# Second layer's modulation: products on TensorE, or a running sum over row tiles on VectorE

## The reference, cut to what matters

```python
for l in range(DEPTH):                               # DEPTH = 2, D = 1024
    mod = silu_c @ w_mod[l] + b_mod[l]               # w_mod[l]: 1024 x 6144
    mod_c = silu_cc @ w_mod[l] + b_mod[l]
    sh1, sc1, g1, sh2, sc2, g2 = jnp.split(mod[:, None, :], 6, axis=-1)
    csh1, csc1, cg1, csh2, csc2, cg2 = jnp.split(mod_c, 6, axis=-1)
    ac = modulate(rms_norm_2(hc, norm1_g[l]), csh1, csc1)
    ...
    h = h + g1 * mix
    h = h + g2 * sq_relu_mlp(modulate(rms_norm_2(h, norm2_g[l]), sh2, sc2), w_ff1[l], w_ff2[l])
    if l < DEPTH - 1:                                # the context leaves after layer 0
        hc = hc + cg1 * mix_c
        ...
```

## Time and profile before

| | us |
|---|---|
| median of 3 timed runs | 2056.79 |
| range of the runs | 2055.26 to 2058.39 |
| span of the profiled execution | 2050.1 |
| TensorE busy in the span | 1990.1 |
| VectorE busy | 1195.2 |
| ScalarE busy | 890.0 |

### The profile page before, as it was taken

One profiled execution on the slowest core, in us unless ns is written; L12 is line 12 of the kernel. 1 busy time (PEld: TensorE's weight loads), 2 busy tenths in 40 slices (PEclk: granted clock), 3 DMA queues, 4 the chain that ended last, 5 costly groups with the idle time before them and its releaser, 6 DMA issues.

```text
span 2050.1 us, 33804 instructions
## 1 busy us (share of the span) xinstructions
PE 1990.1 (97%) x13960; PEld 1728.6 (84%) x13960; DVE 1195.2 (58%) x2137; ACT 890.0 (43%) x1514; POOL 167.0 (8%) x187
## 2 busy tenths in 40 slices
PE   7899999999999999999999999999999999999998
PEld 7768999897889999787788877777778897997887
DVE  6756666776466666425434455444444635677776
ACT  5656544436464444325423333222232426455443
POOL 0220100012021100003410000000000003000000
PEclk9999999999999999899999999999999999999999
DMA  7374699856656665225433325455444421664554
GB/s 233 100 225 146 182 224 224 213 173 188 203 153 180 187 209 164 62 59 163 129 102 93 104 72 185 144 183 165 151 144 153 136 77 37 188 193 144 185 185 134
DMA packets 331751, 317.60 MB, mean 155 GB/s; under 512 B 17077, under 2 KB 315964, under 8 KB 331342
## 3 DMA queue, kind: packets, MB, share of 16 engines
q1 hardware_dynamic: 326580, 301.64, 48.3%
q0 software_dynamic: 3904, 12.03, 2.9%
q10 hardware_dynamic: 1114, 1.76, 0.3%
HBM read 306.54 MB, written 8.85 MB: 154 GB/s over the span
## 4 chain that ended last, share of the span: by engine, by line
PE 87%; DVE 6%; DMA 3%; ACT 2%; issue 1%; POOL 0%; ACTq 0%; SPq 0%; DVEq 0%; POOLq 0%
PE acc L673 20%; PE acc L674 19%; PE acc L675 19%; PE acc L723 7%; PE acc L722 4%; DVE w_low L1963 3%; PE pss L872 2%; PE acc L688 1%; PE acc L719 1%; PE acc L689 1%; PE acc L690 1%; DMA raw<-in_w_mod 1%; PE pst L884 1%; ACT w_high L1421 1%; DMA raw<-in_l_w_down 1%
## 5 line engine op out<-in xcount | busy, mean ns | idle before, releaser
L1963 DVE TENSOR_TENSOR w_low<-raw,w_high 128x1024 fp32r<-128x1024 f32 (+4 forms) x503 | 561.5, 1156 | 151.9 <-ACT w_high L1421 149.3
L1421 ACT ACTIVATE w_high<-raw 128x1024 fp32r<-128x1024 f32 (+4 forms) x503 | 471.9, 984 | 393.8 <-PE acc L675 242.7
L673 PE MATMUL acc<-normed,w_high 128*128 128x256 f32 (+1 forms) x1768 | 568.7, 322 | 0.2
L674 PE MATMUL acc<-normed,w_high 128*128 128x256 f32 (+1 forms) x1768 | 563.4, 319 | 0.0
L675 PE MATMUL acc<-normed,w_low 128*128 128x256 f32 (+1 forms) x1768 | 562.9, 318 | 0.0
L673 PEld LDWEIGHTS acc<-normed,w_high 128*128 128x128 f32 x1768 | 338.4, 191 | 28.7 <-issue 4.4
L675 PEld LDWEIGHTS acc<-normed,w_low 128*128 128x128 f32 x1768 | 338.5, 191 | 22.8
L674 PEld LDWEIGHTS acc<-normed,w_high 128*128 128x128 f32 x1768 | 338.6, 192 | 22.3
L723 PE MATMUL acc<-inner,w_high 128*128 128x512 f32 x612 | 218.1, 396 | 0.0
L673 PE MATMUL acc<-inner,w_high 128*128 128x512 f32 (+2 forms) x576 | 199.2, 346 | 2.2 <-DVE w_low L1963 2.0
L674 PE MATMUL acc<-inner,w_high 128*128 128x512 f32 (+2 forms) x576 | 196.7, 341 | 0.0
(11 more groups left out here) (278 smaller groups left out, 2783.6 us busy)
## 6 DMA issues: line engine op xcount, KB each, us to landing
raw<-in_w_ff SPq DMA_DIRECT2D x128, 512.0 KB, 4.3
raw<-in_w_mod SPq DMA_DIRECT2D x96, 512.0 KB, 4.8
raw<-in_w_in SPq DMA_DIRECT2D x84, 512.0 KB, 4.1
raw<-in_l_w_gate SPq DMA_DIRECT2D x44, 512.0 KB, 5.2
raw<-in_l_w_up SPq DMA_DIRECT2D x44, 512.0 KB, 4.4
raw<-in_l_w_down SPq DMA_DIRECT2D x32, 512.0 KB, 4.7
raw<-in_l_w_qkv SPq DMA_DIRECT2D x24, 512.0 KB, 4.4
raw<-in_l_w_out SPq DMA_DIRECT2D x16, 512.0 KB, 4.6
```

The source lines that it names most:

```text
L673: mm(dst, lh, rh, start=i == 0, stop=False)
L674: mm(dst, lh, rl, start=False, stop=False)
L1421: nc.scalar.activation(WH[:, s % NSPLIT, w0:w0 + nw], RAW[:, r:r + nw], ACT.Copy).then_inc(w_high, 1)
L1963: V.tensor_tensor(WL[:, s % NSPLIT, c], RAW[:, r:r + nw], WH[:, s % NSPLIT, c].bitcast(F32), ALU.subtract).then_inc(w_low, 1)
```

## The change

Layer 0's modulation stays as it is. Layer 1's is computed in another way, in the same stage.

- The loads: `w_mod[1]` now comes as rows. A piece is one row tile (128 rows, one per partition) by 1024 columns, which is one of the six parts `q` (shift 1, scale 1, gate 1, shift 2, scale 2, gate 2). There are 32 late units, one after every ordinary unit of the stage. The first 16 have one piece each (parts 0 and 1, eight row tiles each), the last 16 have two (parts 2 to 5). That is 48 pieces and 25 MB, as before.
- VectorE: for each piece it multiplies the row by the vector's value of that partition and adds it to a running sum in fp32 of 128 by 1024 (L2186 for row tile 0, L2189 for the others). Parts 0 and 1 have two sums, one per vector, parts 2 to 5 one. A piece is free when its last such operation is done.
- TensorE: when a part is complete, at the earliest two units later, each 128 columns of the sum are the stationary operand against one column of ones, which sums over the partitions and leaves the result as a column in `PSO` (`late_columns`, L837): 16 matmuls for parts 0 and 1, 8 for parts 2 to 5. VectorE adds the bias into `MODC` (L2202).
- Gone from the stage: the 24 units of `modulate`, the 12 `columns`, ScalarE's 12 copies and VectorE's 12 reductions with their bias additions.

```diff
+        def mod_sum(q, s):
+            return wk(D * q, D) if s else (view(ROPE, 0, (D,)) if q % 2 == 0 else wk(2 * D, D))
...
-        mod_units = [(l, c) for l in range(2) for c in range(0, 6 * D, 256)]
+        mod_units = [(0, c) for c in range(0, 6 * D, 256)]
...
+        def late_modulation():
+            q, j = (len(late_mods) // 8, len(late_mods) % 8) if len(late_mods) < 16 else \
+                (2 + (len(late_mods) - 16) // 4, 2 * ((len(late_mods) - 16) % 4))
+            n = 1 if q < 2 else 2
+            unit(part(kp(A["w_mod_2"][1])[:, j:j + n, D * q:D * q + D], 0, D), words=n * D, split=False)
+            late_mods.append((q, j, n))
+            ahead.append(len(order) - 1)
...
                     for m in range(0, D, cols):
                         unit(part(kp(A["w_ff2_2"][l])[:, tiles * c:tiles * (c + 1), m:m + cols], 0, cols))
-                        if l == 0 and m == 0:
-                            modulation(1)
-                            ahead.append(len(order) - 1)
+                        if l == 0:
+                            late_modulation()
...
+            def late_columns(steps):
+                while st["late"] < sum(end <= steps - 2 for end in mod_end):
+                    q = st["late"]
+                    if q:
+                        pe.wait_ge(mod_known, q)
+                    pe.wait_ge(mod_added, mod_ready[q])
+                    for s in range(2 if q < 2 else 1):
+                        for c in range(KD):
+                            ins = mm(PSO[:, KD * s + c:KD * s + c + 1], mod_sum(q, s)[:, P * c:P * c + P], ones[:, 0:1],
+                                     start=True, stop=True)
+                    ins.then_inc(mod_summed, 1)
+                    st["late"] += 1
...
                 def step():
                     if l == 0:
-                        modulate((PSO, PSS[0]), PSS[1])
+                        assert not order[st["unit"]][0]
+                        st["unit"] += 1
+                        st["steps"] += 1
+                        late_columns(st["steps"])
...
+            def late_modulation():                     # on VectorE, after each unit's split()
+                q, j, n = late_mods[st["late"]]
+                u = ahead[st["late"]]
+                late_known(sum(end <= st["late"] - 4 for end in mod_end))
+                st["late"] += 1
+                for i in range(len(pieces[u])):
+                    dve.wait_ge(w_full[landed[u, i][0]], landed[u, i][1])
+                    w = RAW[:, raw_at[u, i]:raw_at[u, i] + D]
+                    for s in range(2 if q < 2 else 1):
+                        acc, part = mod_sum(q, s), SILC[:, j + i, s:s + 1]
+                        if j + i == 0:
+                            ins = V.tensor_scalar(acc, w, part, None, ALU.mult)
+                        else:
+                            dve.wait_ge(mod_added, st["added"] - (q < 2))
+                            ins = V.scalar_tensor_tensor(acc, w, part, acc, ALU.mult, ALU.add)
+                        st["added"] += 1
+                        ins.then_inc(mod_added, 1)
+                    raw_free[u, i] = (mod_added, st["added"])
...
+            def late_known(upto):
+                while st["known"] < upto:
+                    q = st["known"]
+                    st["known"] += 1
+                    dve.wait_ge(mod_summed, q + 1)
+                    bm = vcol["b_mod_2"] + 48 + KD * q
+                    for s in range(2 if q < 2 else 1):
+                        ins = V.tensor_tensor(MODC[:, 48 + KD * q:48 + KD * q + KD, s], PSO[:, KD * s:KD * s + KD],
+                                              VEC[:, bm:bm + KD], ALU.add)
+                    ins.then_inc(mod_known, 1)
+                    dve.wait_ge(mod_known, q + 1)
...
                             for i in range(4):
                                 residual_half(2 * i, 48 * l + 40, 0)
                                 if i == 1:
-                                    modulation(len(mod_units) // 2 - 1)
-                            modulation(len(mod_units) // 2)
+                                    late_modulation()
+                            late_modulation()
+                            late_known(5)
                             residual_half(0, 48 * l + 40, 1)
```

More of the change, by code:

```diff
@@ L317, in build @@
         MODS = 8
+        late_mods = []
+        def late_modulation():
[5 more added lines that the diff above has]
+            ahead.append(len(order) - 1)
         FFN_CHUNKS = [(0, 8), (8, 8), (16, 6)]
@@ L389, in build @@
                         unit(part(kp(A["w_ff2_2"][l])[:, tiles * c:tiles * (c + 1), m:m + cols], 0, cols))
-                        if l == 0 and m == 0:
-                            modulation(1)
-                            ahead.append(len(order) - 1)
-        assert len(mod_used) == len(mod_units)
+                        if l == 0:
+                            late_modulation()
+        assert len(mod_used) == len(mod_units) and late_mods[-1] == (5, 6, 2)
         split_ids = [i for i, u in enumerate(order) if u[0]]
@@ L553, in build @@
         skew_w = sem("skew_w")
+        mod_added, mod_summed, mod_known = sem("mod_added"), sem("mod_summed"), sem("mod_known")
         bias_in = sem("bias_in")
@@ L566, in build @@
         raw_free = {}
+        mod_ready = [16, 32, 40, 48, 56, 64]
+        mod_end = [sum(q <= p for q, j, n in late_mods) for p in range(6)]
         pair_bank, cols_bank = {}, {}
@@ L632, in _ @@
             st = {"phase": 0, "acc": 0, "unit": 0, "split": 0, "task": 0, "sq": 0, "freed": 0, "store": 0,
-                  "pair": 0, "rope": 0, "spread": 0}
+                  "pair": 0, "rope": 0, "spread": 0, "late": 0, "steps": 0}
             mm = nc.tensor.matmul
@@ L996, in last_product @@
                 turned(wb, four, x, 4, S)
-                all_columns()
+                step()
                 turned(wa, four[0:2], far, 4, S)
@@ L1009, in last_product @@
                 split_free[a] = (acc_full, st["acc"])
-                turned(wb, four, far, 4, S)
+                turned(wb, four[0:2], far, 4, S)
+                late_columns(len(late_mods) + 2)
+                turned(wb, four[2:4], far, 4, S)
                 split_free[b] = (acc_full, st["acc"])
@@ L1308, in _ @@
                                 project(1, hidden(c, T), T, m=cols // P, kt=tiles)
-                            if m == 0:
-                                step()
+                            step()
                             if last and m:
@@ L1855, in _ @@
                 tiles = 2048 // T
-                steps = 2 * st["pair"]
                 for kind, c in ffn2_turns(T):
@@ L1859, in _ @@
                         for m in range(0, tiles, 2):
-                            if l == 0:
-                                modulation_rows((steps - 1) // 2)
-                                steps += 1
                             if l:
@@ L1935, in _ @@
             st = {"phase": 0, "chain": 0, "acc": 0, "task": 0, "rot": 0, "sig": 0, "split": 0, "store": 0, "mod": 0,
-                  "relu": 0, "turned": 0, "spread": 0}
+                  "relu": 0, "turned": 0, "spread": 0, "late": 0, "added": 0, "known": 0}
             go = lambda: fence(dve, st)
@@ L2071, in mod_gain @@
                 m = 48 * l + 24 * which + 8
-                for s in range(2):
+                for s in range(1 if l and which else 2):
                     link(V.scalar_tensor_tensor(MGAIN[:, which, :, s], MODC[:, m:m + 8, s], 1.0,
@@ L2591, in _ @@
                 tiles = 2048 // T
-                steps = 2 * st["mod"]
                 for kind, c in ffn2_turns(T):
-                    if l == 0 and kind == "out":
-                        modulation((steps - 2) // 2)
-                        steps += 1
                     if kind == "in":
                         for m in range(0, tiles, 2):
-                            if l == 0:
-                                modulation((steps - 2) // 2)
-                                steps += 1
                             if l:
@@ L2650, in _ @@
                             residual_half(4, 48 * l + 40, 1)
+                            late_known(6)
                             residual_half(6, 48 * l + 40, 1)
```

8 lines of the change are left out of this document (removed).

## The result

The changed kernel takes 2070.45 us (2068.98 to 2073.46, 4 runs) against 2057.59 before (2055.26 to 2058.5, 4 runs on the same chip): ratio 1.0069, 95% interval 1.0054 to 1.0083. It is 0.7% slower; 2039 was forecast. What was written down as the fourth case, with 9 in 100, is what happened: VectorE's late release holds back the ordinary weights, at a loop of 13 us or more.

A forecast was written before the change was run, and what follows sets the result against it. TensorE was taken to bound the stage: 33.8 us off, 9.2 added, net 24.6, less 3.7 stall and 2.9 last turn, 18.0 off 2050.1; with 6.7 around it, 2039 us, 8 in 10 range 2030 to 2057.

The forecast's parts named there:

- the fourth case: Slower rival: VectorE's late release holds back the ordinary weights in the second half; landing 5.6, 2067 us, chance 0.09.
- VectorE's prices: Running-sum steps on VectorE: 1.28 us each, 0.75 for row tile 0, 78 us in total.
- What goes from TensorE: Insertions and transpositions leaving TensorE in the stage: 36.0 us, of which 33.8 in the first 30 units.
- The loop: Second half's turn of sums, loads, high and low part: mean 11.3 us against TensorE's 10.87; stall 3.7 us.
- The step that failed: Second half's four piece landings, counted from x: +4.9, +6.3, +7.7 and +9.1 us, with next x at +11.4.
- x: End of the second low part in a unit; allowed to slide to 7.4 us after TensorE's unit end.
- my own rival's arithmetic: Sum in the fourth case: loop 13.3 us, excess 2.4 x 14 = 34, less 1.9 of room: 32 us stall.
- The columns: One-column matmuls added to TensorE: 56 before the last turn at 0.165 us, 9.2 us; ends 4.6 and 11.8.
- The 64-column row: Profile row behind the matmul price: one moving, 64 stationary columns, four matmuls in 0.33 us, doubled to 0.165 each.
- The clock: Sign on TensorE: the mechanism is wrong if its clock, 1.00 in the stretch, falls; no time was assigned.
- The last turn: Stage's end, where the norm counts: reciprocal at +21.6 instead of +18.7 us after TensorE's preceding unit, 2.9 later.
- The rival "TensorE alone decides": Second half's loads land quicker, loop 10.9 us, nothing stalls: 25.3 us gain, time 2031.5, chance 0.27.

The follow-up runs named there:

- run 15: Changed kernel with late w_mod pieces cut to the first 512 of 1024 columns, rows still 24 KB apart: 2041.37 us, 0.9938.
- run 3: Changed kernel with the second layer's w_mod rows loaded in 1-KB packets, four to a row, in reverse order: 2076.35 us, 1.0099.
- run 12: Changed kernel with each late w_mod piece loaded as a block of 4 row tiles by 256 columns, the shape of before: 2069.17 us, 1.0063.
- run 14: Changed kernel with late w_mod pieces read from w_o_2, each 512 KB in one dense stretch of DRAM: 2065.85 us, 1.0054.
- run 5: On top of run 2, 8 matmuls of eight columns each in place of the 64 one-column matmuls: 2023.79 us, 0.984.
- run 6: On top of run 2, each part's one-column matmuls spread over two units, the last part's as before: 2035.16 us, 0.9897.
- run 11: Changed kernel with each part's one-column matmuls spread over two units, VectorE's order as it was: 2066.52 us, 1.0052.
- run 2: Changed kernel with VectorE's w_mod sums ahead of the low parts of the ordinary weights, load order unchanged: 2037.83 us, 0.9914.

## Why the prediction was wrong

**Right.** VectorE's prices: a sum was forecast at 1.28 and 0.75 us, and the trace has 1.28 and 0.75 (L2189 1280 ns, L2186 749). What goes from TensorE: 33.8 forecast before the last turn, 32.7 measured. The loop, its members and its order were named, and the second half as its place. The first half runs at TensorE's pace, as forecast.

**The step that failed** is the time of the four landings in the ring: "its place filled +4.9; second sum done +2.6, filled +6.3; the two ordinary pieces queued behind them +7.7 and +9.1". From x = 1440.1 the trace has them at +5.0, +9.0, +10.2 and +11.5, so the next x comes at +13.8 and not at +11.4. The first landing was right and the second came 2.7 late; the two behind it keep a distance of 1.3 each and are late with it. So it is in the mean of the 11 bursts from 1441 to 1579: 3.8, 7.2, 8.7 and 10.2 us after the first issue, where my steps make 3.7, 5.1, 6.5 and 7.9. I took 1.4 us a piece from a stretch at 370 GB/s and one piece after the other. The burst at 1441.4, cut at its first two landings and its last (us busy by engine, then granted clock, DMA share, GB/s):

```profile
1441.40:1445.10 3.70, 3.70 (x18) 3.07 (x17) 2.27 (x3) 1.23 (x2) 0.00 (x0) 1.00 0.58 176
1445.10:1449.10 4.00, 4.00 (x19) 3.31 (x18) 0.64 (x2) 0.60 (x1) 0.00 (x0) 1.00 0.92 306
1449.10:1451.60 2.50, 2.50 (x12) 2.06 (x11) 1.22 (x3) 1.70 (x2) 0.00 (x0) 1.00 0.23 88
```

When the second piece has landed, 1.9 of the 2.1 MB have moved, most of them at 306 GB/s: the pieces move together, and the last 2.5 us are a tail at a DMA share of 0.23. Over the whole burst it is 206 GB/s. Run 15 gives the price of bytes directly: 0.5 MB less brings the mean of the last landing from 10.2 to 7.7 us after the first issue, 2.5 us where my steps make 1.4. Runs 3, 12 and 14 exclude packet size, shape and distance of the rows. Why the last bytes of a piece come so late stays open.

At a loop of 13.7 my own rival's arithmetic applies, with one correction: it put 32 us of stall at 13.3, and the trace has 16 of gaps. Column steps and half clock lengthen TensorE's units too, in the second half by 5.2 and 7.8, and the loop's excess is counted against them first; together that is 29.

That the right case stood among the rivals, at a landing of 5.6, is in part luck: it was reached by a later first landing, and the first landing was on time.

**The columns** were taken at 0.165 and cost 0.21 to 0.22: five steps 12.4 for 9.2. The 64-column row that I followed was no guide for 128; the L833 row and the Trainium skill's rule (TensorE: Matmul & The Clock Gate, LDWEIGHTS) were, at 0.21. Here the measurement sides with the rule that I set aside, and run 5 confirms it: 14.0 us less, against 12.2 for 56 matmuls and 1.7 for one stretch of half clock.

**The clock** was in no term. I said that a fall would break the mechanism; it fell to 0.50 for 3.4 us at a time at three column steps and for 6.8 and 10.2 at the stalls, and cost 11.2 us. The batch of 16 is the cause at the first two steps (runs 5, 6 and 11 against the rest); at the third, a step of 8 with a gap of 1.0 us behind it, the cause was not tested.

**The last turn** was forecast 2.9 later for the norm. The unit before the turn ends on TensorE at E = 1594.7, and VectorE, late with its sums, empties the last bank only at 1595.4. So x = E + 8.5 (7.4 forecast), and the reciprocal ends at E + 25.2 and not 21.6, 6.5 later than before: the late landings again, and 1.7 of a column step that I had counted ahead of the turn. In run 2, whose x is early, the reciprocal ends 17.7 us behind the turn's first product, where before it was 18.7.

**The rival "TensorE alone decides"** was near what the change can do (2035 to 2038 with VectorE's order turned, against 2031.5), not what it did. The Trainium skill's rule for a load that spoke for it (DMA: Bandwidth & Descriptors, Anatomy of one DMA: 2.0 us and the bytes at 436 GB/s, 3.2 us here) is 0.6 under the 3.8 of a piece that is first in an idle queue and far from the 5.8 of the second (means of the 11 bursts). What I did not ask is which piece VectorE reaches first. The order on VectorE was free, and the place of one call in two loops stood between 2070 and 2038.

The fastest kernel that leaves nothing out is run 6 (0.9897), with run 2 (0.9914) not distinguishable from it; both beat the kernel before and the changed one.

## What to carry to other kernels

Where several streams share a ring of buffers and one queue of loads, let each engine take the pieces in the order in which they land: an engine that handles a late piece first holds back the early ones whose places the next loads need, and the loop then contains the whole burst. Before pricing such a loop, price a burst's last landing by a burst of the same bytes, not by the first landing plus the peak rate. And gaps on every engine with none of them full, and ScalarE waiting for a load that waits for VectorE, were here the sign of such a loop, not of too much work.

## What the runs showed of the hardware that was not expected

- At a batch of 16 matmuls with one moving column (3.6 us with TensorE busy throughout) the granted clock falls to 0.50, that is to 1.2 GHz, for 3.4 us in 13 of 13 profiled executions at the second batch, and for 3.4 or 6.8 us in 11 of 13 at the first. Where the 16 were spread over two units, or left out, the clock stayed at 1.00 there (3 of 3).
- Four loads of 512 KB issued within 2.3 us land on average 3.8, 5.8, 7.0 and 7.9 us after their issues (11 bursts of the changed kernel); with the first two at 256 KB 2.7, 3.3, 4.5 and 5.4 (12 bursts of run 15).
- A scalar_tensor_tensor of 64 columns takes 281 ns, one of 1024 columns 1280.
